# Feed-forward operands made from row differences: their transposes laid under the sample rows' product and the first weight block, samples side by side, one key bias loaded first

## The reference, cut to what is computed

```python
D_MODEL, SEQ, DEC_SEQ, PAST_LEN = 1024, 1024, 32, 1024
D_FF = -(-8 * D_MODEL // (3 * 256)) * 256            # 2816
...
s = jnp.einsum('bqhd,bshd->bhqs', qb, k) * scale      # forgetting attention, one query block
s = s + cq[..., None] - ct[:, :, None, :]             # the last term is the key bias
...
h = layer_norm(ALPHA * x + mix @ w_out, g1, b1)       # "mix" stage
y = layer_norm(ALPHA * h + (silu(h @ w_gate) * (h @ w_up)) @ w_down, g2, b2)
```

## Time and profile before

| | |
|---|---|
| median of 3 runs | 1507.0 us (1504.52 to 1508.43) |
| the profiled execution | 1505.24 us, of which its span, the time the profile covers, is 1503.5 us |
| mean TensorE clock granted | 0.973 of full speed |
| busy: PE, PE weight loads, VectorE, ScalarE, GpSimd | 94%, 83%, 55%, 44%, 41% |
| mix stage, last product to first feed-forward product | 747.2 to 777.2 us |

### The profile page before, as it was taken

The page is one execution under the profiler, slowest core; times in us unless marked ns, Lnnn a source line. Parts: engine busy times, 40 slices in busy tenths (PEclk is TensorE's granted clock), DMA queues, the critical chain, the costliest instruction groups (busy, mean ns, idle before and its releaser), DMA issues.

```text
span 1503.5 us, 23326 instructions
## 1 busy us (share of the span) xinstructions
PE 1407.1 (94%) x8976; PEld 1247.7 (83%) x8976; DVE 825.6 (55%) x1588; ACT 669.0 (44%) x1252; POOL 616.7 (41%) x620
## 2 busy tenths in 40 slices
PE   6999989988998799899959999999999999999998
PEld 6869889976776577678749999999999998876886
DVE  3279999796884898734663333333333343114525
ACT  4467878826884788810153222222222243213121
POOL 3421424542331022323275555555555566412043
PEclk9999999998999899989969999999999999999999
DMA  6101213239944031421101222222221236523341
GB/s 227 47 11 58 63 58 100 72 86 208 226 140 121 9 93 44 140 85 43 46 28 57 85 72 72 85 86 86 86 77 67 85 112 207 173 84 112 112 156 58
DMA packets 99998, 141.99 MB, mean 94 GB/s; under 512 B 18360, under 2 KB 76440, under 8 KB 99888
## 3 DMA queue, kind: packets, MB, share of 16 engines
q1 hardware_dynamic: 99888, 140.51, 30.6%
HBM read 106.28 MB, written 24.23 MB: 87 GB/s over the span
## 4 chain that ended last, share of the span: by engine, by line
PE 53%; DVE 1%; POOL 1%; issue 0%; ACT 0%; POOLq 0%; DVEq 0%; ACTq 0%
PE ffn L2459 30%; PE ffn L2094 7%; PE ffn L2476 5%; PE ffn L2478 5%; PE ffn L2477 5%; PE ffn L2499 1%; PE ffn L2501 1%; POOL h_T_lo L2662 0%; POOL w_lo L2635 0%; DVE h_T_even L2716 0%; POOL down_lo L2657 0%; DVE h_T_odd L2716 0%; DVE h_B_lo L2719 0%; ACT h_B_hi L2557 0%; DVE rows L2035 0%
## 5 line engine op out<-in xcount | busy, mean ns | idle before, releaser
L2635 POOL TENSOR_TENSOR w_lo<-w_S,w_hi 128x512 fp32r<-128x512 f32 x88 | 120.8, 1373 | 99.5 <-ACT w_hi L2534 99.5
L2459 PE MATMUL ffn<-h_T_hi,w_hi 128*128 128x264 f32 x704 | 143.5, 285 | 0.0
L2459 PE MATMUL ffn<-h_T_lo,w_hi 128*128 128x264 f32 x704 | 143.1, 285 | 0.0
L2459 PE MATMUL ffn<-h_T_hi,w_lo 128*128 128x264 f32 x704 | 142.2, 283 | 0.0
L2476 PE MATMUL ffn<-down_hi,act_hi 128*128 128x512 f32 x352 | 138.4, 393 | 0.4 <-POOL down_lo L2657 0.4
L2478 PE MATMUL ffn<-down_hi,act_lo 128*128 128x512 f32 x352 | 138.3, 393 | 0.0
L2477 PE MATMUL ffn<-down_lo,act_hi 128*128 128x512 f32 x352 | 138.2, 393 | 0.0
L2534 ACT CAST w_hi<-w_S 128x512 fp32r<-128x512 f32 x88 | 54.7, 622 | 180.4 <-PE ffn L2459 178.6
L2657 POOL TENSOR_TENSOR down_lo<-down_raw,down_hi 128x1024 fp32r<-128x1024 f32 x32 | 80.5, 2522 | 106.5 <-ACT down_hi L2593 78.0
L2735 DVE TENSOR_TENSOR act_lo<-act_raw,act_hi 128x512 fp32r<-128x512 f32 x44 | 37.5, 857 | 147.3 <-ACT act_hi L2601 147.3
L2459 PE MATMUL ffn<-h_B_hi,w_hi 128*128 128x264 f32 x528 | 108.7, 287 | 6.5 <-DVE h_B_lo L2719 6.5
(11 more groups left out here) (372 smaller groups left out, 3927.9 us busy)
## 6 DMA issues: line engine op xcount, KB each, us to landing
down_raw<-in_w_down SPq DMA_DIRECT2D x38, 512.0 KB, 3.7
act<-gated SPq DMA_DIRECT2D x11, 1056.0 KB, 4.1
gate_raw<-in_w_gate SPq DMA_DIRECT2D x11, 1024.0 KB, 5.3
up_raw<-in_w_up SPq DMA_DIRECT2D x11, 1024.0 KB, 5.4
act_raw<-act SPq DMA_DIRECT2D x44, 256.0 KB, 2.8
w_raw<-in_w_in SPq DMA_DIRECT2D x9, 1024.0 KB, 5.5
x_raw<-in_xT SPq DMA_DIRECT2D x8, 528.0 KB, 8.3
key_bias<-scratch_negc SPq DMA_DIRECT2D x8, 512.0 KB, 5.5
```

The source lines that it names most:

```text
L2459: mm = nc.tensor.matmul(pp[:, bank[to] + ch, 0:PIECE], l, x[name][:, k, ch * PIECE:(ch + 1) * PIECE], start=opens and k == 0 and i == 0, s ...
L2635: nc.gpsimd.tensor_tensor(w_lo[n % 2][:, :, :], weight(m, SCHEME[q][0]), f32(w_hi[n % 2][:, :, :]), ALU.subtract).then_inc(w_lo_done, 1)
```

## The change

It does five things.

1. SyncE loads the key bias of head 2 ahead of the stacking of head 3 and the sample bias' store.
2. MIX_ORDER becomes 1, 5, 2, 6, 3, 7, 0, 4, samples, so that a pair is complete every second tile. Each tile is normalised before the next tile's residual add.
3. The sample rows' product has 32 matmuls in place of 48: high and low part stand side by side (64 columns) against the weight's high part, and the high part alone against its low part. It is cut in four quarters of 8, each behind the 12 transposes (B11, B21, B22) of a tile pair. ScalarE copies the lower half out of PSUM (copy_lower), and VectorE adds it.
4. T1 to T4 of the prompt are made by GpSimd as differences of untransposed rows (16 of 128 x 512), and PE transposes them too. ScalarE rounds them and VectorE makes their low parts straight from PSUM. The sample's T stay as they were, on 64 columns.
5. The first pass takes its blocks in the order A11, S1, S2, A12, S3, A22, S4. Its first two blocks are multiplied by the 256 prompt columns first and by the 8 sample columns later, and the transposes of T2, T3 and T4 stand between halves of blocks. `up_raw` is loaded after the last of them; the sums S1 to S4 of the second pass come after C21.

```diff
@@ fox, SyncE @@
+            if b % 2 == 1 and b // 2 + 2 < FOX_H:
+                biased(b // 2)
+                load_bias(sp, b // 2 + 2)
             if b == 0:
...
                 sp.dma_start(d["bias_s"][:, 0:PAST], bias_s[:, :]).then_inc(bias_stored, 16)
-            if b % 2 == 1 and b // 2 + 2 < FOX_H:
-                biased(b // 2)
-                load_bias(sp, b // 2 + 2)
@@ mix stage @@
-MIX_ORDER = [1, 2, 3, 4, 5, 6, 7, 0, NT]
+MIX_ORDER = [1, 5, 2, 6, 3, 7, 0, 4, NT]
+    def sample_quarter(pe, quarter):
+        half = quarter // 2
+        cols = slice(512 * half, 512 * half + 512)
+        if quarter == 0:
+            pe.wait_ge(pre_done, NT - 1)
+        for k in range(quarter % 2 * KH, quarter % 2 * KH + KH):
+            nc.tensor.matmul(py[0:2 * NEW, cols], mT_s[:, k, :], w_hi[:, k, cols], start=k == 0, stop=False,
+                             skip_group_check=True)
+            mm = nc.tensor.matmul(py[0:NEW, cols], mT_s[:, k, 0:NEW], w_lo[:, k, cols], start=False, stop=k == KD - 1,
+                                  skip_group_check=True)
@@ transition, PE @@
+            for j in range(4):
+                transposes("B", j)
+                sample_quarter(pe, j)
+            for j in range(4):
+                transposes("T1", j)
+            every, first, second = range(KH), range(KH // 2), range(KH // 2, KH)
+            pe.wait_ge(w_lo_done, 1)
+            pe.wait_ge(h_lo, lowered_at("B", 3))
+            products(0, 0, every, "prompt")
...
+            products(1, 3, first, "prompt")
+            sample_transposes()
+            products(1, 3, second, "prompt")
+            pe.wait_ge(h_lo, lowered_at("S", "B"))
+            products(0, 0, every, "samples").then_inc(product_done, 1)
+            for j in range(4):
+                transposes("T2", j)
...
@@ transition, GpSimd: T4 of pairs 0 and 1 follow split(2) likewise, those of 2 and 3 split(3) @@
+            first_differences(pool, 3)
+            split(0)
             split(1)
+            differences("T2", 0)
+            differences("T2", 1)
+            differences("T3", 0)
+            differences("T3", 1)
+            norm1.root(pool, NT, NEW, NT)
...
@@ transition, VectorE @@
+            for j in range(4):
+                lows("B", j)
+            mix_weights(0, ("S1",))
+            evicted(dve, NT)
+            for j in range(4):
+                lows("T1", j)
+            sample_centred(dve)
+            mix_weights(0, ("S2",))
+            sample_shifted(dve)
+            sample_lows()
@@ SyncE @@
-            sp.wait_ge(t_lo, 16)
+            sp.wait_ge(h_tr, transposed("T4", 3))
             load(1)
```

More of the change, by code:

```diff
@@ L2079, in tensor @@
     def tensor(pe):
-        for n, t in enumerate(MIX_ORDER):
-            rows = TILES[t][2]
+        for n in range(NT):
             pe.wait_ge(m_lo, n + 1)
@@ L2121, in mix_lo @@
             pool.wait_ge(m_hi, n + 1)
-            nc.gpsimd.tensor_tensor(mT_lo[n % 2][:, :, 0:rows], mT[:, :, r0:r0 + rows],
-                                    f32(mT_hi[n % 2][:, :, 0:rows]), ALU.subtract).then_inc(m_lo, 1)
+            high, low = (mT_hi[n % 2], mT_lo[n % 2]) if n < NT else (mT_s, mT_s[:, :, NEW:2 * NEW])
+            nc.gpsimd.tensor_tensor(low[:, :, 0:rows], mT[:, :, r0:r0 + rows], f32(high[:, :, 0:rows]), ALU.subtract)\
+                .then_inc(m_lo, 1)
         mix_lo(1)
-        for n, t in enumerate(MIX_ORDER):
-            norm.root(pool, n, TILES[t][2], n)
-            if n + 2 <= NT:
+        for n in range(NT):
+            norm.root(pool, n, P, n)
+            if n + 2 < NT:
@@ new lines, in products @@
+            def products(n, q, ks, part):
+                _, name, to = SCHEME[q]
+                opens = q in (0, 1, 3, 5)
+                for k in ks:
+                    wh, wl = w_hi[n % 2][:, k, :], w_lo[n % 2][:, k, :]
+                    for i, (l, x) in enumerate([(wh, hi), (wh, lo), (wl, hi)]):
+                        flags = {"start": opens and part != "samples" and k == 0 and i == 0, "stop": k == KH - 1 and i == 2,
+                                 "skip_group_check": True}
+                        rows = {"prompt": slice(0, 2 * P), "samples": slice(2 * P, PIECE), "all": slice(0, PIECE)}[part]
+                        for ch in range(2):
+                            mm = nc.tensor.matmul(pp[:, bank[to] + ch, rows], l,
+                                                  x[name][:, k, ch * PIECE + rows.start:ch * PIECE + rows.stop], **flags)
+                return mm
@@ new lines, in _ @@
+            pe.wait_ge(h_lo, lowered_at("T2", 3))
+            products(2, 1, first, "all")
+            transposes("T3", 0)
+            transposes("T3", 1)
+            products(2, 1, second, "all").then_inc(product_done, 1)
+            transposes("T3", 2)
+            transposes("T3", 3)
+            pe.wait_ge(w_lo_done, 4)
+            pe.wait_ge(p1_copied, 1)
+            products(3, 2, first, "all")
+            transposes("T4", 0)
+            transposes("T4", 1)
+            products(3, 2, second, "all").then_inc(product_done, 1)
@@ L2565, in _ @@
+            split(2)
+            for j in range(4):
+                highs("T2", j)
+            keep_p1(0)
+            split(3)
+            for j in range(4):
+                highs("T3", j)
+            split(4)
+            for j in range(4):
+                highs("T4", j)
+            split(5)
+            silu(0, "C11", 0)
+            split(6)
+            silu(0, "C22", 1)
+            split(7)
+            silu(0, "C21", 2)
+            split(8)
+            for m in range(1, NM):
                 for q in range(NQ):
```

403 lines of the change are left out of this document (267 added, 136 removed).

## The result

The changed kernel is slower: 1513.8 us median of 8 runs (1510.26 to 1522.01) against 1507.38 us of 8 runs of before, ratio 1.0047 with the interval 1.0033 to 1.0061, so about 7 us.

What follows compares the result with a forecast made beforehand. PE, busy 94% of the span, was taken to bound the kernel. Gains of 3.0 us in the transition and 2.5 in attention made 5.5 off the profiled 1505.24: 1499.7, as a median 1501.5 us, range 1497 to 1506.5.

Steps and rivals of the forecast that it cites:

- the transition: From the last prompt tile to the eighth feed-forward block: 5.2 us gained, less 1.6 and 0.6 for the clock, 3.0 net.
- the longer gap: PE's idle time before the sample's transposes, waiting for the sample's normalisation: forecast at 9.5 us.
- 1.6 + 0.6: Clock losses counted in us: 1.6 after the 9.5 us gap, 0.6 allowed for the 3.0 us gap at 742.5.
- the waits of 1.0 and 0.6: PE waits in us around the first two blocks, for the sample's low parts and another low part; expected to absorb slow-clock loss.
- the price of the small matmuls: The first two blocks' 48 matmuls of 8 columns: 0.06 us each, 1.45 us per 24.
- my other end: The upper price considered for an 8-column matmul: 0.122 us, as for 264 columns.
- Back at work, before needed 5.5 us at half speed, 2.7 lost ... Here 1.6 lost.: After the 9.5 us gap: slow-clock loss of 1.6 us, part of the earlier 2.7 being absorbed by waits.
- POOL takes the port again (1.25) before DVE's last pass.: Before the sample's transposes: one more POOL difference, 1.25 us, precedes DVE's last sample pass of 1.3 us.
- the third twelve: The third group of 12 transposes after the last prompt tile: PE idle 3.0 us for the first pair's low parts.
- So both waits go: 2.5 gained.: Attention stage: loading the key bias earlier removes DVE's 3.32 and PE's 2.52 us waits, gaining 2.5 us.
- slow-clock rival: Clock falls at the 742.5 gap and stays low until the steady blocks: 12 us lost, 1512.5 us; chance 0.07.
- the first gap: PE's 3.0 us idle time at 742.5; its clock loss was left open: nothing or 2.5 to 3.3 us, 0.6 allowed.

Runs made afterwards that it cites:

- e4: The changed kernel with its 48 matmuls of 8 columns widened to 264 columns; ratio 1.0012 to the kernel before.
- e6: The changed kernel with GpSimd's differences waiting for VectorE's last sample pass, and its T1 difference for the last prompt tile's second pass; ratio 1.0005 to before.
- e8: The kernel before with 96 matmuls of 8 columns added ahead of the 41st feed-forward block; ratio 1.0125 to before.
- e9: The kernel before with 96 matmuls of 264 columns added ahead of the 41st feed-forward block; ratio 1.0083 to before.
- e3: The changed kernel without 44 of its 48 matmuls of 8 columns; ratio 0.9982 to the kernel before.
- e2: The changed kernel with one GpSimd wait added, so the differences after the sample's root follow VectorE's last sample pass; ratio 1.0006 to before.
- e14: The changed kernel with three tiny VectorE operations between the sample's root and its last pass; ratio 1.0051 to the kernel before.
- e1: The kernel before with only the key bias of head 2 loaded first; ratio 0.9996 to before.
- e7_sample_first: The changed kernel with the sample's product ahead of all transposes, first two blocks unsplit, VectorE and GpSimd reordered to it; ratio 0.9985 to before.
- e5: The changed kernel with GpSimd's differences waiting for VectorE's last sample pass and the first two blocks unsplit; ratio 0.9994 to before.
- e10: e7_sample_first with VectorE's low parts of B before the sample's passes, and GpSimd's difference after the last prompt tile's second pass; ratio 0.9970 to before.

## Why the prediction was wrong

The sum was 5.5 us off the profiled time; it came out 9.5 above it. Of these 15.0 us, 12.2 lie in the transition (9.2 longer where 3.0 shorter was forecast), 1.5 in attention and ahead of it, 1.4 behind. Term by term the 12.2 are, within a microsecond: 7.2 more for the small matmuls; 2.6 for the longer gap; 4.8 for the low level on all other work (half of 10.6 us behind 771.4 and half of 3.4 at 744.4, 7.0, where 1.6 + 0.6 were counted); less 1.6 for the waits of 1.0 and 0.6, which didn't come.

- **The step that failed first: the price of the small matmuls**, "I take 0.06, since its columns are the nearer". They cost 0.112 at full clock, near my other end, and 0.213 at half: 10.1 us for 2.9. Of the 7.2 between, 2.5 are the price and 4.7 the low level. The pair in the earlier trace rows lies 0.06 apart, probably because its weights are loaded under the 384-column matmuls ahead of it (the load for the first of the pair begins at 366.30, its matmul at 366.47), a cover that a row of small ones doesn't have; I had no row of small ones among small ones. That the weight load sets the price of 0.112 is my reading; no run changed the load alone. The Trainium skill, TensorE: Matmul & The Clock Gate, Back-to-back issue gap, gives about 81 ns per matmul for a stream with 128 columns and weight loads; the runs here show 112 for 8 columns.
- **The step that cost most: "Back at work, before needed 5.5 us at half speed, 2.7 lost ... Here 1.6 lost."** The level stayed low through 20.7 us of work and not 5.5. I had taken the time that it needed behind 264-column work for that of any work. e4, e6, e8 and e9 show that a row of 8-column matmuls, PE busy throughout, takes the level away where the same row with 264 columns leaves it or brings it back. Ahead of that row six kernels do the same 3.7 us of work (the sample's transposes and half a block), and whether the level is back by its end differs for a reason that no run isolates: in e3 it was back after 3.7 us and in e6 after 3.9; in the changed kernel, e2, e4 and e14 it was not. In the three of these with the 24 small matmuls it stayed low through the whole row; in e4, with the wide ones, it came back some 3 us into it.
- **"POOL takes the port again (1.25) before DVE's last pass."** The mechanism was right, the number of turns wrong: four, not one. Without them the wait is 4.6 us shorter (e2), of which I had counted one turn, 1.25, and the distance another 2.7. The other waits came about as worked out: 2.7 for 3.0 at the third twelve, the root 1.2 late.
- **"So both waits go: 2.5 gained."** They went, and the key biases behind took it back (e1). In the changed kernel's own execution, matched matmul by matmul with before, PE gains 3.1 us by 366 and loses 0.2 of it by 381, 0.5 at 408 and 1.2 at 424; and 0.8 of the 1.2 us by which the mix stage begins earlier stood there already at 345, ahead of the moved load. I had looked for what is late next among the stacked operands and not at the next loads of the same kind.
- The slow-clock rival had 0.07. Its size came (1512.5 for 1513.8) by luck, its place did not: at the first gap the level was low for 3.4 us only. The weighing of transposes in it was wrong as well. The Trainium skill, TensorE: Matmul & The Clock Gate, Part 4: PE-mode transpose, says that they don't count as busy like matmuls. In e7_sample_first PE took up work with 16 transposes and nothing else, and the level came back at 770.17, in the midst of them:

```profile
767.43 3.27 PE L2521 MATMUL ffn<-ident,rows_T 128*128 128x128 f32 x16 [8.99 <-DVE h_B_lo L2940]
```

- So transposes did bring the level back here, and the measurement decides; whether they are in the mode that the page speaks of, no row shows. Not every row of them did: in e2_shift_first it returned at 779.8, in the midst of T2's transposes and behind 24 small matmuls, while the changed kernel's same 16 (780.1 to 783.4) left it low. Windows of e2, small ones and then transposes:

```profile
771.70:776.90 5.20, 5.20 (x27) 5.20 (x27) 2.96 (x6) 0.00 (x0) 1.40 (x2) 0.50 0.00 0
776.90:780.20 3.30, 3.30 (x20) 3.30 (x19) 1.38 (x2) 2.32 (x4) 2.46 (x3) 0.56 0.00 0
```

- The up_raw load was never waited for. The 1.4 us more in the down products stand almost wholly in one place (at 1381 of the changed kernel's profile), where PE waits 0.75 and 0.17 us for low parts of down_raw, a load that ScalarE there waits 3.92 us for and before 1.72. The same shows, smaller, in most of the other kernels made from the changed one, hardly in e5's and e10's (0.2) and not in e1's. It was not tried, and stays open.
- Two slips that decide nothing: by my own durations 8 transposes and half a block are 2.3 us and not 2.0; and the row that I gave for L2719 beside POOL (760.50) stands where POOL was idle, though in the same trace those at 752.55 and 753.75, with POOL busy, take 0.68 too.

## What to carry to other kernels

A narrow matmul with weights of its own costs nearly as much as a wide one (0.112 us for 8 columns, 0.122 for 264), and a row of them can cost the clock besides: fill a gap with it only if the gap would have been longer than the row at half speed. Where an engine shares a port with another, give the pass that others wait for its own place in the other engine's order, by a wait if need be. When a wait for one buffer of a rotation is removed, look first at the next turn of the same rotation.

## What the hardware showed that I had not expected

- In the dense feed-forward, 96 matmuls of 8 columns took 18 us and those of 264 columns 11.8: less work was slower.
- The granted clock fell from 1.00 to 0.50 under a PE that was busy throughout, 2.4 us after the first small matmul (898.2 to 900.6 in the clock's record).
- A VectorE pass with its operands in SBUF took 5.86 us, through four GpSimd subtractions of 1.23, where it took 1.27 with GpSimd kept waiting; another such pass waited for one. Issued 0.2 us later it still ended behind the fourth.
- 16 transposes alone brought the granted clock from 0.50 back to 1.00 in 2.7 us (767.43 to 770.17 in e7_sample_first).
